# A streaming encoder layer on eight cores: the first instructions moved ahead of the program branch, sixteen up-projection chunks of the samples done early, and mixing steps moved from VectorE to GpSimd

## What is computed

```python
h = rms_norm(x, norm1_g)
g_b, g_c, x_a, x_l, g_l = split(h @ w_in)          # five parts of 512 channels
out_a = g_b * conv3_causal(g_c * x_a)              # mixer A
c = conv4_causal(x_l) + b
r, i = sigmoid(c @ wa + ba), sigmoid(c @ wx + bx)  # block-diagonal gates
log_a = -8 * r * softplus(a_param); a = exp(log_a)
h_t = a_t * h_(t-1) + sqrt(1 - a_t**2) * (i_t * c_t)   # mixer B, a recurrence over time
out_b = h_t * gelu(g_l)
x = x + concat(out_a, out_b) @ w_out
x = x + square(relu(rms_norm(x, norm2_g) @ w_up)) @ w_down
y = rms_norm(x, norm_f_g)
```

## Time and profile before

| | us |
|---|---|
| median of the 3 runs shown | 998.66 |
| lowest, highest | 908.91, 1062.85 |
| the profiled execution | 909.05 |
| its slowest core (6, first program), first to last instruction | 907.5 |
| even cores (first program) | 903.0 to 907.5 |
| odd cores (second program) | 899.8 to 902.1 |

### The profile page before, as it was taken

The page is one execution under the profiler, slowest core; times in us unless marked ns, Lnnn a source line. Parts: engine busy times, 40 slices in busy tenths (PEclk is TensorE's granted clock), DMA queues, the critical chain, the costliest instruction groups (busy, mean ns, idle before and its releaser), DMA issues.

```text
span 907.5 us, 15041 instructions; the slowest of 8 cores (899.8 to 907.5 us)
## 1 busy us (share of the span) xinstructions
PE 839.3 (92%) x4392; PEld 428.5 (47%) x4464; DVE 425.2 (47%) x722; ACT 376.3 (41%) x754; POOL 184.9 (20%) x307
## 2 busy tenths in 40 slices
PE   2679789699999999999999999999999899999995
PEld 2444345255564444444444444555445455446542
DVE  4698886663301210636665434575315477514112
ACT  4578738552331000554942134583205485205301
POOL 4132240234453000232100013120003212003200
PEclk9799889899999999999999999999999999999998
DMA  8999999999888534685553369565248852778751
GB/s 237 205 180 215 214 117 130 134 180 177 163 182 168 145 96 126 241 318 172 141 149 84 117 164 300 163 166 161 84 151 254 267 159 73 233 198 271 206 163 73
DMA packets 80441, 158.26 MB, mean 174 GB/s; under 512 B 9184, under 2 KB 9312, under 8 KB 80352
## 3 DMA queue, kind: packets, MB, share of 16 engines
q1 hardware_dynamic: 61632, 111.76, 42.4%
q0 software_dynamic: 15264, 33.30, 23.2%
q10 hardware_dynamic: 3456, 12.14, 4.1%
HBM read 165.75 MB, written 32.57 MB: 219 GB/s over the span
## 4 chain that ended last, share of the span: by engine, by line
PE 82%; DMA 8%; DVE 4%; issue 3%; ACT 2%; POOL 0%; POOLq 0%; DVEq 0%; ACTq 0%; SPq 0%
PE ps L1037 28%; PE ps L1087 27%; PE ps L780 12%; PE ps L989 7%; DMA sb_ring<-wscr 4%; PE ps L776 3%; DMA sb_uT<-wall 3%; PE ps L1079 2%; PE ps L697 1%; PE ps L1097 1%; DMA sb_xsl<-xp 1%; PE ps L855 1%; ACT sb_t_rig L532 1%; PE ps L1074 1%; DVE sb_t_xc L882 1%
## 5 line engine op out<-in xcount | busy, mean ns | idle before, releaser
L1037 PE MATMUL ps<-sb_hT,sb_ring 128*128 128x512 bf16 (+2 forms) x1050 | 194.3, 341 | 6.2 <-DVE sb_a_pb L535 4.3
L532 ACT ACTIVATE sb_junk<-sb_xsl 128x1024 bf16<-128x1024 f32 (+1 forms) x59 | 59.6, 1010 | 269.7 <-DVE sb_xsl L535 256.6
L535 POOL TENSOR_TENSOR sb_uT<-sb_rl 128x512 bf16<-128x512 bf16 (+1 forms) x80 | 83.0, 1038 | 418.4 <-ACT sb_stat L532 272.7
L532 ACT ACTIVATE sb_rl<-ps 128x512 bf16<-128x512 f32 (+2 forms) x192 | 98.1, 525 | 142.2 <-PE ps L1037 127.8
L1037 PEld LDWEIGHTS ps<-sb_hT,sb_ring 128*128 128x128 bf16 x1064 | 104.4, 99 | 91.3 <-issue 8.4
L535 DVE TENSOR_TENSOR sb_xsl<-ps,sb_xsl 128x512 f32<-128x512 f32 (+1 forms) x60 | 46.1, 794 | 200.7 <-PE ps L1087 139.9
L1087 PE MATMUL ps<-sb_ring,sb_uT 128*128 128x512 bf16 x576 | 138.5, 379 | 0.8
L1087 PE MATMUL ps<-sb_uS,sb_uT 128*128 128x512 bf16 x423 | 95.7, 379 | 0.5
L1037 PE MATMUL ps<-sb_hT,sb_uS 128*128 128x512 bf16 (+1 forms) x466 | 92.6, 354 | 0.3
L1087 PEld LDWEIGHTS ps<-sb_ring,sb_uT 128*128 128x128 bf16 x592 | 57.6, 98 | 67.8
L780 PE MATMUL ps<-sb_hT,sb_ring 128*128 128x512 bf16 (+1 forms) x369 | 81.8, 367 | 5.0 <-DMA sb_ring<-wscr 4.6
(11 more groups left out here) (100 smaller groups left out, 841.7 us busy)
## 6 DMA issues: line engine op xcount, KB each, us to landing
sb_ring<-wscr SPq DMA_DIRECT2D x240, 256.0 KB, 3.5
sb_uS<-wscr SPq DMA_DIRECT2D x160, 256.0 KB, 3.0
wscr<-wall POOLq DMA_DIRECT2D x64, 256.0 KB, 10.8
sb_xsl<-xp ACTq DMA_DIRECT2D x18, 512.0 KB, 8.7
yp<-sb_xsl POOLq DMA_DIRECT2D x13, 512.0 KB, 7.9
sb_uT<-wall POOLq DMA_DIRECT2D x16, 256.0 KB, 24.1
wscr<-sb_uT SPq DMA_DIRECT2D x16, 256.0 KB, 14.4
sb_wout<-wout POOLq DMA_DIRECT2D x4, 512.0 KB, 13.1
```

The source lines that it names most:

```text
L532: return OP("act", dur, lambda e: e.activation(out=out, in_=in_, func=func, **kw), rd_, wr_)
L535: return OP(eng, dur, lambda e: e.tensor_tensor(out=out, in0=in0, in1=in1, op=op), rd_, wr_)
L1037: return lambda slot: [lambda e, kc=kc: e.matmul(out=bank_ap(b, q.N), lhsT=slot[:, kc * 128:(kc + 1) * 128], rhs=h_ap(q, True, kc, 0, q.N) ...
```

## The change

Four things:

1. **Common beginning.** The generator steps that both programs share are emitted first (`lead`) and stand ahead of the register load and branch (`cut` holds how many of each list): the parameter DMA, four DMAs of x, the first four weight chunks, the constants and one more DMA of POOL. For this the first six 512 KB pieces of x of either program are laid in one input, `head`, with the same place in both; they are loaded as 2, 2, 1 and 1 pieces.
2. **Samples' up chunks.** In the second program S's matmuls of w_up chunks 16 to 31 (`MORE`) are emitted as soon as S's second norm is there, without the token "retired", at the low priority of the MLP; M0's loop leaves them out and later loads these chunks again. The weight order is turned so that chunks 16 to 31 are converted first. The memset that frees M0's memory no longer covers the half of `uS` that they write.
3. **First program**: i times xc, the gelu product and the first step of mixer A's convolution go from DVE to POOL.
4. **Second program**: r = a a is a POOL multiplication in place of ACT's exponential.

```diff
     def make(name):
         def f(e):
+            n = cut[name]
+            put(e, arms[0].prog[name][:n])
             r = e.alloc_register("side")
             e.reg_load(r, side[0:1, 0:1])
             with e.If_eq(r, 0):
-                put(e, name, arms[0])
+                put(e, arms[0].prog[name][n:])
...
+    def lead(self, gen, n):
+        s, val = Strand(gen, -99, 0), None
+        pace, self.PACE = self.PACE, {}
+        while n:
+            s.req, val = gen.send(val), None
+            if s.req[0] == "get":
+                val = s.req[1].take(s.req[2])
+            else:
+                self._emit(s, self._start(s.req))
+                n -= 1
+        self.PACE = pace
...
+        def g_head():
+            for k, n in ((0, 2), (2, 2), (4, 1), (5, 1)):
+                yield DMA("act", xsl[:, k * D:(k + n) * D], head[:, k * D:(k + n) * D], [], [xsl_b[k + i] for i in range(n)], "x", 0.52 * n)
...
-                yield MSET("pool", uS[:, 0:1], 0.0, uS_b[::4] + [hT_b[NHT]])
+                yield MSET("pool", uS[:, 0:1], 0.0, uS_b[0:16:4] + [hT_b[NHT]])
...
-            yield ACT(0.69 * f, r, r, AF.Exp, [T["b_r"], der_b], [T["b_r"]], scale=nsp2[:, c:c + 1])
+            if second_half:
+                yield TT("pool", 1.2 * f, r, a, a, ALU.mult, [T["b_a"]], [T["b_r"]])
+            else:
+                yield ACT(0.69 * f, r, r, AF.Exp, [T["b_r"], der_b], [T["b_r"]], scale=nsp2[:, c:c + 1])
...
-            yield TT("dve", 0.66 * f, i_, i_, xc, ALU.mult, [T["b_i"], T["b_xc"]], [T["b_i"]])
+            yield TT("dve" if second_half else "pool", (0.66 if second_half else 1.2) * f, i_, i_, xc, ALU.mult, [T["b_i"], T["b_xc"]], [T["b_i"]])
...
-                yield TT("dve", 0.66 * f, gl, gl, x2, ALU.mult, [T["b_gl"], T["b_x2"]], [T["b_gl"]])
+                yield TT("dve" if second_half else "pool", (0.66 if second_half else 1.2) * f, gl, gl, x2, ALU.mult, [T["b_gl"], T["b_x2"]], [T["b_gl"]])
...
-            yield TS("dve", 0.5 * f, ya3, pb3[:, :, 0:L], caw[:, c:c + 1], None, ALU.mult, None, [pbb, par_b], [A["b_ya"]])
+            yield TS("dve" if second_half else "pool", (0.5 if second_half else 1.1) * f, ya3, pb3[:, :, 0:L], caw[:, c:c + 1], None, ALU.mult, None, [pbb, par_b], [A["b_ya"]])
...
+            early = range(32 - MORE, 32) if second_half and t is Ms[0] else ()
...
+            for fc in early:
+                (b,) = yield get(P_bank, 1, 2)
+                yield PER(8 * 0.11, up(Ss, b), [hT_b[Ss.h2]], [bank_b[b]], CH_UP + fc)
+                W.spawn(g_relu(Ss, fc, b), -5)
             if t is Ms[0]:
-                yield tok("projM0", 20)
+                yield tok("retired")
...
+        if second_half:
+            order[20:52] = [CH_UP + (fc - MORE) % 32 for fc in range(32)]
+        setup, conv, pars, rows = g_setup(), g_conv(order), g_par(), g_head()
+        for gen, n in ((pars, 1), (rows, 4), (conv, 4), (setup, 8), (conv, 1)):
+            W.lead(gen, n)
+        cut = {e: len(S.prog[e]) for e in S.ENG}
```

More of the change, by code:

```diff
@@ L20 @@
 AHEAD = 6
+MORE = 16
 FIRST = (512, 512, 512, 384, 384)
@@ L143, in check_no_deadlock, with emit, put @@
             raise RuntimeError("static deadlock: " + "; ".join(msg))
-def emit(nc, arms, side):
-    def put(e, name, S):
-        for waits, fns, inc in S.prog[name]:
+def emit(nc, arms, cut, side):
+    def put(e, part):
+        sem = arms[0].sem
+        for waits, fns, inc in part:
             for k, v in waits:
-                e.wait_ge(S.sem[k], v)
+                e.wait_ge(sem[k], v)
             ins = None
@@ L645, in arm @@
         chain = Ls[0:1] + [Ss] + Ls[1:] + Ms
+        assert [t.J if not t.lean else 4 for t in chain[:2]] in ([4, 2], [2, 4])
         def xap(k):
@@ L1051, in g_mlp @@
                 bs = []
-                qs = ts if fc >= len(ahead) else [t]
+                qs = ts if fc >= len(ahead) and fc not in early else [t]
                 for q in qs:
@@ L1167, in arm @@
         order = [12, 13, 14, 15] + [16, 8, 4, 0, 17, 9, 5, 1, 18, 10, 6, 2, 19, 11, 7, 3] + list(range(CH_UP, NCHUNK))
-        W.spawn(g_setup(), -20)
-        W.spawn(g_conv(order), 500)
-        W.spawn(g_par(), -19)
-        W.spawn(g_xloads(), -10)
+        if second_half:
+            order[20:52] = [CH_UP + (fc - MORE) % 32 for fc in range(32)]
[3 more added lines that the diff above has]
+        cut = {e: len(S.prog[e]) for e in S.ENG}
+        for gen, prio in ((setup, -20), (conv, 500), (pars, -19), (rows, -11), (g_xloads(), -10)):
+            W.spawn(gen, prio)
         W.spawn(g_norm1s(), -1)
@@ L1225 @@
         rows[:len(mine)] = mine
+        wide = f(np.concatenate([x_prompt[s, a:a + n].reshape(n, 8, 128).transpose(2, 1, 0).reshape(128, 8 * n)
+                                 for a, n in zip(np.cumsum((0,) + SKIP), SKIP)], axis=1))
+        few = tall(x_sample[4 * c:4 * c + 4].reshape(256, D))
         st = np.concatenate([sca[4 * c:4 * c + 4].reshape(8, 512), slc[4 * c:4 * c + 4].reshape(12, 512), slh[4 * c:4 * c + 4]], axis=0)
@@ L1230 @@
             "xp": rows,
-            "xl": f(np.concatenate([x_prompt[s, a:a + n].reshape(n, 8, 128).transpose(2, 1, 0).reshape(128, 8 * n)
-                                    for a, n in zip(np.cumsum((0,) + SKIP), SKIP)], axis=1)),
-            "xs": f(x_sample[4 * c:4 * c + 4].reshape(256, D)),
+            "xl": wide,
+            "head": f(np.concatenate([wide[:, :4096], few] if hf else [few, tall(rows[:512])], axis=1)),
             "side": np.full((1, 1), hf, np.int32),
```

25 lines of the change are left out of this document (17 added, 8 removed).

## The result

| | before | after |
|---|---|---|
| median of all runs, us | 911.02 | 913.68 |
| ratio, 95% interval | | 1.0044 (1.0031 to 1.0056) |
| the profiled execution: even cores, us | 903.0 to 907.5 | 909.1 to 912.2 |
| odd cores, us | 899.8 to 902.1 | 903.1 to 910.5 |

The change made the kernel 0.4% slower, 4 us, where I forecast a ratio of 0.996. It is inside the 2% band that got 0.86, but the sign is the other one, and the interval leaves no doubt of it.

A forecast was written before the change was run, and what follows sets the result against it. Core 6's first program decides, limited before 180 us by DVE's backlog and the DMA engines. 907.5 - 1 (beginning) - 2.7 (steps to POOL) = 903.8, plus 1.55 outside the span: 905.4 us, ratio 0.996; range 892 to 920.

The forecast's parts named there:

- the 2% band that got 0.86: Whole kernel: measured time within 2% of no change, 890.9 to 927.2 us; chance 0.86.
- What happens on other engines there is covered: Core 6, 180 to 700 us: PE busy 516.3 of 520 us, so a cheaper DVE step is worth nothing.
- The term for the stage before 180 us: Core 6, 20 to 180 us: three steps moved to POOL gain net 2.7 us; ends -16 and +11.
- I take nothing for it: First program: each block's path grows 0.4 to 1.5 us, mostly hidden by three buffer sets; uncovered, 12 us.
- The sum for DVE: Core 6, 20 to 180 us: DVE gives up 16.0 us and loses 13.3, 0.49 of POOL's 27.2.
- They now follow, and cover themselves by transfers under way.: Start: register load and branch hide behind the first DMAs; gain 1 us on core 6, 7.5 on core 7.
- rival 4: Start: beginning gives core 6 nothing or takes something, as core 7 starts together; 906 to 909, within the forecast's 0.55.
- My sign for it: Start: first weight DMA near 1 us on both cores, with about 250 GB/s on both.
- The second program: Core 7: 902.1 less 7.5 for the beginning, less 14.6 for early chunks, plus 5 for r = a a: 885 us.
- just 26 us: Core 7, 20 to 307 us: DMA share 0.91 leaves room for loading sixteen chunks twice, 4 MB, about 26 us.
- Rival 5: Second program becomes the slowest, needing 20 us of loss there above all its ends (895); chance 0.02.
- Rivals 2 and 3: Core 6: lock with DVE slows 40 to 180 us, 919, chance 0.15; POOL's conversions held up, 917, chance 0.10; together 929.

The follow-up runs named there:

- the late tiles alone: Kernel with beginning and early chunks, its order kept, first program's three steps on POOL only for M1 to M4: ratio 1.0082, 10.9 us.
- the early tiles: Kernel with beginning and early chunks, its order kept, first program's three steps on POOL only for samples and M0: ratio 1.0110, 13.4 us.
- both engines at work: Kernel with beginning and early chunks; DVE keeps its three steps, POOL does three extra of the same kinds in dead buffers: ratio 1.0184.
- Two kernels whose lists agree in both programs: Changed kernel with every part undone (only x pieces differ): 1.0011; the same with one memset waiting for half the samples' buffer: 1.0010.

## Why the prediction was wrong, step by step

**The step that failed: "What happens on other engines there is covered".** I read PE's 516.3 of 520 us busy rightly as no room for a gain, and then used it for the other direction too. A stretch in which PE is never idle has nothing to win from a faster DVE; whether it has slack for a slower one is another question, and the table can't answer it. I had seen DVE busy 41% of it and not that its work comes in bursts. In the changed kernel 33 weight loads, 6.5 us, were lost from 400 to 700, and some 3.5 us more after; the late tiles alone cost 10.9 us in an order that doesn't allow for it. The term for the stage before 180 us failed as well: with the order held fixed, the move that was to give 2.7 us there costs 5.5.

**"I take nothing for it" (the path of a block).** Its uncovered price in the text was 12 us. In the order planned for DVE the early tiles cost 13.4 us, disturbance and POOL's list in it. The three buffer sets don't cover it by themselves; an order that allows for the longer steps halves the loss, and that order was the one thing in the change that I did not price. With the steps on DVE it is worth nothing much (0.9947 against 0.9962), but with them on POOL it takes 1.5%, 14 us, off the loss (1.0227 against 1.0077), and so the time until 180 us came out near the forecast, by luck: PE is idle 29.4 us of the stage for my 32, by an order that I had not priced and not by DVE's relief.

**The sum for DVE: nearly the right product of two wrong factors.** The run with the changed kernel's lists and the steps on DVE gives it without anything else moved. From 20 to 180 DVE gave up 16.3 us (forecast 16.0). POOL took 39.8 us for them, not 27.2: the bf16 row was the wrong neighbour for float32 (1.38 and 1.52 us), and a multiplication by a column isn't cheaper than a product of two tiles there but dearer, 2.21 us in this stage where DVE's own takes 0.48. DVE is busy 131.3 us against 131.8, so it lost 15.7 of the 16.3 (forecast 13.3), which is 0.39 of POOL's time and not 0.49. Net 0.6 us in place of 2.7. POOL was busy 78.5 us of the stage, over my 68.

**"They now follow, and cover themselves by transfers under way."** The opposite: behind the transfers the load and branch take longer, 9.98 us on core 6 for 2.66 with nothing under way. The sentence on the Trainium skill's "Runtime: NRT & Kernel Launch" ("Instruction fetch mechanics": a taken branch to code that isn't there waits for a DMA) stood right there in the prediction, and I used it to explain core 7's 9.44 us instead of asking what that DMA would queue behind. The traces agree with it on core 7, whose instruction queues moved 10 packets by 22 us. On core 6 they record no such packet, so the page does not explain its 9.98 us, and what does stays open. The term came out at -0.7 to +2.1 us (three pairs of kernels, none clear of its intervals) for my -1, because the late first matmul is nearly all made up later; rival 4, that it gives core 6 nothing or takes something, is what happened, by another mechanism. My sign for it, the first weight DMA near 1 us on both cores and some 250 GB/s, was met (1.58 us, 255 GB/s from 8 to 12) and said nothing about what stood behind the branch. Nor were core 6's 306 GB/s owed to a silent neighbour: from 12 to 16 us it still moved 313 beside core 7's 208. Why PE makes up 7 us I can't show. In the pair with the POOL steps it happens from 400 us on; in the other two pairs the weight loads are level within 4 at 180 us already (714 against 716, 752 against 748), though in the first of them core 6 is 18 behind at 400 again.

**The second program** (forecast 885; odd cores 905.9, core 7 910.5). The beginning gave 6.9 and 5.5 us in two pairs (forecast 7.5), but 0.4 in the changed kernel. The chunks gave 2.5 and 3.9 us (forecast 14.6): the "just 26 us" of free transfer were not free in the right place. And r = a a cost 12.2, 12.8 and 9.3 us on average over the odd cores, 20.7 on core 7, for my +5. Part of that is a row of core 7, ACT's wait for the product that stands in the middle of its chain, total us, times, longest, 20 to 400 us:

```profile
ACT sb_t_rig L549 <- POOL sb_t_rig L552: 11.6, 12, 2.3
```

I had priced POOL's 28 us, DVE's share of it and ACT's gain, and not the hand-over from ACT to POOL and back in each of 40 blocks. Rival 5 needed 20 us of loss above all my ends and had 0.02; core 7 came within 1.7 us of it.

**Rivals 2 and 3** were right in kind: both engines at work cost 20 us, about 11 by reads that hold DVE up and about 9 by POOL's list. I gave them too little since the net 2.7 us rested on nothing but the middle of a range of -16 to +11. (Together they would have been 919 + 12 = 931, not the 929 in the prediction.)

**Left open:** why the order planned for POOL gives even cores at 896.5 with r = a a beside it and 900.6 without; why the two products alone cost more (1.0196) than all three, and why the even cores lie so far apart there; why the first tap disturbs DVE so little; what holds core 6 up at the load and branch; and how PE makes up the seven microseconds.

## What to carry to other kernels

PE busy all the time in a stage means that a cheaper step on another engine gains nothing there; it does not mean that a dearer one is free, so price a move for all the places where the instruction runs, and look at the engine's busy share inside a burst, not over the stage. Of the 40.9 us that the three steps took off VectorE 36 came back, 0.37 us for each microsecond that GpSimd spent on them. The steps differ: the two products in front of the scan gave all of theirs back and cost 2.3%, the first tap gave back a quarter and cost nothing. So move one step at a time and compare the engine's whole busy time. GpSimd's memsets, which don't read SBUF, left VectorE nearly alone (428.8 us busy against 427.3), but whatever stands behind them in GpSimd's list still comes later (9 us here).

## What the runs showed of the hardware

**A register load and branch are dearer behind a burst of DMAs.** From the last instruction ahead of them to the first behind them POOL took 2.66 us on core 6 with nothing under way (the run with the branch first) and 4.93 to 9.98 us in the fourteen kernels with the beginning ahead. On core 7 it took 9.38 us with the branch first, while core 6's transfers were under way, and 11.49 to 16.58 in the fourteen. Core 7 fetched code in that time; on core 6 no fetch is recorded. The kernel with the branch first had its first matmul 7.5 us earlier. The spread among kernels with the same beginning is not explained.

**The two cores of a pair hang together though they exchange nothing.** Five pairs of kernels with the same lists for the first program, even cores, mean us:

| the second program gets | even cores |
|---|---|
| the early chunks (branch first) | 904.5 to 900.6 |
| the early chunks (beginning ahead) | 909.3 to 901.4 |
| r by ACT in place of POOL | 910.5 to 913.3 |
| r by ACT, steps on DVE | 896.5 to 900.6 |
| r by ACT, order planned for DVE | 902.7 to 901.4 |

Two kernels whose lists agree in both programs (1.0011 and 1.0010) have 904.5 and 906.7, so 2 us mean nothing; but the first three pairs are borne out by their ratios, which the even cores set (1.0011 to 0.9970, 1.0034 to 0.9962, 1.0044 to 1.0077). Some pairs were measured on two chips, on which the kernel before differs too (even cores 906.5 and 903.9 us on average in the sessions of the second pair), so the ratios are the better measure: by them an edit of one core's program is worth 3 to 6.5 us on the other. In the traces of three pairs it shows as longer or shorter waits of core 6's PE for ring slots between 140 and 300 us (9.2 to 3.7 us, 0.2 to 4.6, none to 4.9, the first, third and fourth pair); in the second, the largest, these waits are alike (5.3 and 4.9). That both cores' weights come by the same way at that time is my reading of it; no run here separates them.

**GpSimd's memset is slow too:** 0.61 us for 512 values (1.82 for three), so even clearing a buffer there takes its list for as long as a DVE product.
